# Feed-forward stage of a decoder layer: top-row products of the first pair ahead, splits in order of use, a place of its own for two gated blocks, and a down-projection over eight banks

## The reference, cut to what matters

```python
up = causal_dwconv(rms_norm(h, g_ffn[l]) @ w_up[l], w_conv[l], b_conv[l])   # 2 x 2816 channels, 3 taps
a, b = up[..., :D_FF], up[..., D_FF:]
h = h + (jax.nn.silu(a) * b) @ w_down[l]
return rms_norm(h, g_final)
```

## Time and profile before

| | us |
|---|---|
| median of 3 runs (lowest to highest) | 1912.57 (1912.17 to 1915.29) |
| the profiled execution, its own time | 1916.99 |
| its span in the trace | 1915.2 |
| TensorE busy | 1834.9 (96%) |
| VectorE, ScalarE, GpSimd busy | 951.7, 667.8, 953.6 |

### The profile page before, as it was taken

One profiled execution on the slowest core, in us unless ns is written; L12 is line 12 of the kernel. 1 busy time (PEld: TensorE's weight loads), 2 busy tenths in 40 slices (PEclk: granted clock), 3 DMA queues, 4 the chain that ended last, 5 costly groups with the idle time before them and its releaser, 6 DMA issues.

```text
span 1915.2 us, 25387 instructions
## 1 busy us (share of the span) xinstructions
PE 1834.9 (96%) x8924; PEld 1525.2 (80%) x8924; DVE 951.7 (50%) x1420; ACT 667.8 (35%) x1161; POOL 953.6 (50%) x519
## 2 busy tenths in 40 slices
PE   6999999999997999999999999899999999699998
PEld 6788888888886788878888877588888888588887
DVE  5355454000016566774345445677778787632212
ACT  6422223121013566621233223544444444322212
POOL 6833333456654776334532332567777777533220
PEclk9999999999998899999999999999999999899999
DMA  6511111353322887173221232234343433554312
GB/s 251 198 45 34 34 42 44 137 179 123 93 83 84 318 318 270 45 271 103 99 67 56 66 132 89 94 111 131 115 131 115 131 108 127 188 166 131 103 51 88
DMA packets 72667, 237.95 MB, mean 124 GB/s; under 512 B 6800, under 2 KB 17168, under 8 KB 69264
## 3 DMA queue, kind: packets, MB, share of 16 engines
q1 hardware_dynamic: 48720, 159.31, 25.5%
q10 hardware_dynamic: 23872, 77.60, 11.0%
HBM read 172.93 MB, written 63.96 MB: 124 GB/s over the span
## 4 chain that ended last, share of the span: by engine, by line
PE 64%; POOL 12%; issue 12%; DVE 5%; ACT 5%; DMA 1%; POOLq 0%; ACTq 0%; SPq 0%; DVEq 0%
PE ps L559 19%; PE ps L564 18%; PE ps L565 18%; POOL wl L488 8%; POOL zB L495 2%; PE ps L917 2%; ACT prow L1530 2%; PE ps L894 1%; PE ps L1215 1%; PE ps L1217 1%; PE ps L1216 1%; DVE aneg L2220 1%; DMA raw<-in_slabs 1%; POOL zA L495 0%; PE ps L1045 0%
## 5 line engine op out<-in xcount | busy, mean ns | idle before, releaser
L456 POOL TENSOR_SCALAR wh<-raw 128x1024 fp32r<-128x1024 f32 x76 | 211.7, 2786 | 533.4 <-PE ps L559 510.5
L559 PE MATMUL ps<-uh,wh 128*128 128x512 f32 (+1 forms) x576 | 228.6, 397 | 2.4 <-POOL wl L458 2.4
L565 PE MATMUL ps<-uh,wl 128*128 128x512 f32 (+1 forms) x576 | 225.5, 391 | 0.0
L564 PE MATMUL ps<-ul,wh 128*128 128x512 f32 (+1 forms) x576 | 225.1, 391 | 0.0
L458 POOL TENSOR_TENSOR wl<-raw,wh 128x1024 fp32r<-128x1024 f32 x76 | 183.0, 2408 | 6.3
L488 POOL TENSOR_TENSOR wl<-raw,wh 128x512 fp32r<-128x512 f32 x88 | 140.0, 1611 | 35.3 <-ACT wh L1228 35.3
L535 POOL TENSOR_TENSOR wl<-raw,wh 128x1024 fp32r<-128x1024 f32 x28 | 71.4, 2551 | 141.6 <-ACT wh L1228 141.6
L1907 DVE SCALAR_TENSOR_TENSOR ya<-zA,sm,ya 128x512 f32<-128x512 f32 x88 | 93.8, 1066 | 89.3 <-ACT ya L1762 80.8
L475 POOL TENSOR_TENSOR over_rings<-over_rings 128x512 f32<-128x512 f32 x88 | 113.4, 1289 | 44.1 <-DMA over_rings<-in_slabs 38.8
L1907 DVE SCALAR_TENSOR_TENSOR yb<-zB,sm,yb 128x512 f32<-128x512 f32 x88 | 127.7, 1451 | 14.4 <-ACT yb L1762 8.2
L1228 ACT ACTIVATE wh<-raw 128x512 fp32r<-128x512 f32 (+1 forms) x124 | 90.5, 749 | 115.3 <-PE ps L559 78.0
(11 more groups left out here) (434 smaller groups left out, 4855.4 us busy)
## 6 DMA issues: line engine op xcount, KB each, us to landing
raw<-in_slabs SPq DMA_DIRECT2D x134, 512.0 KB, 3.6
over_rings<-in_slabs SPq DMA_DIRECT2D x22, 1024.0 KB, 7.0
s_s<-over_rings SPq DMA_DIRECT2D x22, 1024.0 KB, 4.8
ssm<-s_s SPq DMA_DIRECT2D x22, 512.0 KB, 3.7
raw<-s_s SPq DMA_DIRECT2D x22, 512.0 KB, 4.7
s_f<-yb ACTq DMA_DIRECT2D x22, 512.0 KB, 2.6
fs<-s_f ACTq DMA_DIRECT2D x22, 512.0 KB, 3.5
a<-in_slabs SPq DMA_DIRECT2D x22, 256.0 KB, 2.6
```

What stands on the lines that cost most here:

```text
L456: pool.tensor_scalar(wh[:, j, :], raw[:, j % RAWS, :], 1.0, None, ALU.mult).then_inc(S["w_hi"], 1)
L559: l = pe.matmul(o, lh, rh, start=start, stop=False)
L564: pe.matmul(o, lh, rl, start=False, stop=False)
L565: return pe.matmul(o, ll, rh, start=False, stop=stop)
```

## The change

Five things are moved; no arithmetic is added or removed.

1. Pair 0 on TensorE: VA11 waits for bank 0 alone; VA12 comes second (both use f0), and the order is VA11, VA12, VS2, VS1, VS3, VS4, VA22. So that VA12 can be added into bank 0, TensorE waits for ScalarE's copy of VA11.
2. Before it, VectorE takes out half 0 of the last `w_xo` block ahead of `mixed(2)`, and the high parts and differences of t2, t1, t3, b2 and t4 are written out in one list each (HIS, LOS). t4's high parts no longer stand behind the copy of the 1/rms rows.
3. Gated blocks 4 and 5 get a staging tile fs4 of their own; their loads wait for VA12 of the last pair (fs4 lies on f0h). VectorE takes the differences of 0, 2, 3 and 4, GpSimd those of 1 and 5.
4. The down-projection uses all eight banks: block m is in banks 2(m mod 4) and the next. Group 0 computes blocks 0 to 3 of its operands for m = 0 and m = 1 first, then operands 4 and 5 for both (`first_two`). The waits for a free bank look three blocks back.
5. The wait for the last gated block's store goes from in front of the weight splits to the load of gated block 6. The transposes of the final gain are moved behind block 0 of group 2, into banks 4 and 5.

```diff
+FIRST = (VA11, VA12, VS2, VS1, VS3, VS4, VA22)
+HIS = [("t2", 0), ("t2", 1), ("t2", 2), ("t3", 0), ("t3", 1), ("t1", 0), ("t2", 3), ("t1", 1), ("t3", 2), ("t1", 2),
+       ("t3", 3), ("t1", 3), ("b2", 0), ("b2", 1), ("b2", 2), ("b2", 3), ("t4", 0), ("t4", 1), ("t4", 2), ("t4", 3)]
+LOS = [("t2", 0), ("t2", 1), ("t2", 2), ("t1", 0), ("t2", 3), ("t1", 1), ("t1", 2), ("t1", 3),
+       ("b2", 0), ("b2", 1), ("b2", 2), ("b2", 3)]
...
+        (fs4,) = place(72, [("fs4", [P, 2, T], 0)])
...
-            round_of(FB - 1, (lambda: (down(0), f_lo(1)), lambda: (f_lo(3), down(1))))
+            round_of(FB - 1, (lambda: (down(0), f_lo(1), down(1), f_lo(5)), lambda: None))
             scaled_by(FB, "zb0", zB, 0, v_at(FB, "c21"))
-            f_lo(5)
...
                 if first:
-                    for b in range(2):
-                        pe.wait_ge(d_free[b], FF_USE0)
-                elif second_:
+                    pe.wait_ge(d_free[0], FF_USE0)
+                    product(i, VA11, q, f0h, f0l, ready=made("o_gl", lambda k: KB + k + 1))
+                    pe.wait_ge(S["f_a"], a_at(0, "p1c"))
+                    product(i, VA12, q, f0h, f0l, CH, more=True, ready=made("o_gl", lambda k: KB + CH + k + 1))
+                    pe.wait_ge(d_free[1], FF_USE0)
+                    product(i, VS2, q + 1, t2h, t2l, ready=made("xT_lo", lambda k: lo_at("t2", k)))
+                    sums(1, ach, acl)
...
+            def first_two():
+
+
+                pe.wait_ge(S["f_v"], v_at(FB - 1, "c21"))
+                for ks in (range(CH), range(CH, FGROUPS[0])):
+                    for m in range(2):
+                        if ks[0] == 0:
+                            pe.wait_ge(S["w_ready"], s + m + 1)
+                        for b in range(2):
+                            for k in ks:
...
+                        if g == 0 and isinstance(i, int) and i == 0:
+                            pe.wait_ge(S["f_v"], v_at(FB - 1, "c12") if j == 2 else v_at(FB, "c21"))
+                            dense(j, s + j, 0, G, blocks(g), freed=2 if j == 2 else 1, bank=2 * j)
+                            continue
+                        if g == len(FGROUPS) - 2 and isinstance(i, int) and i == 0 and j == 2:
+                            pe.wait_ge(S["rb_c"], 3)
+                        dense(j, s + 4 * i + j, u + 4 * i + j - 3, G, blocks(g), bank=2 * j)
...
+                    if m == KB - 1 and b == 1:
+                        act.wait_ge(d_done[1], USE0["xo"] + KB)
+                        parts(0, 3)
                     square(1, m, b, USE0["xo"], hF, sq, f0h, "g_ffn")
...
+                if m == KB - 1:
+                    p1_copy(0, 0)
...
-                if c in (4, 5):
-                    act.wait_ge(*((S["f_p"], F_AT[1]) if c == 5 else (S["xT_lo"], 2 * KB + 3 * CH + 1)))
+                if c == 4:
+                    act.wait_ge(S["p_done"], NV * (FB - 1) + VA12 + 1)
+                elif c == 6:
+                    act.wait_ge(S["g_st0"], ST0 + 16 * FB)
...
             gated_out(FB)
-            act.wait_ge(S["g_st0"], ST0 + 16 * FB)
...
+            evac(0)
+            mixed(2)
...
-            quarters(n, 1, (lambda: f_lo(2, 0, 2),))
+            quarters(n, 1, (lambda: (f_lo(2, 0, 2), f_lo(3, 0, 3)),))
+            f_lo(4, 0, 4)
             rest_of(FB, 0)
-            f_lo(4, 0, 4)
```

More of the change, by code:

```diff
@@ L1126, in seven, with made @@
                 q = 4 * e
-                def made(sem_, n):
-                    return (lambda k: pe.wait_ge(S[sem_], n + k + 1)) if first else None
+                def made(sem_, at):
+                    return lambda k: pe.wait_ge(S[sem_], at(k))
                 def after(name, n=i):
@@ L1133, in seven @@
                 if first:
-                    for b in range(2):
-                        pe.wait_ge(d_free[b], FF_USE0)
-                elif second_:
+                    pe.wait_ge(d_free[0], FF_USE0)
[5 more added lines that the diff above has]
+                    sums(1, ach, acl)
+                    product(i, VS1, q + 2, t1h, t1l, ready=made("xT_lo", lambda k: lo_at("t1", k)))
+                    product(i, VS3, q + 3, t3h, t3l, ready=made("f_p", lambda k: k + 1))
+                    rms_rows(1)
+                    after("u4")
+                    product(i, VS4, q + 2, b2h, b2l, more=True, ready=made("xT_lo", lambda k: lo_at("b2", k)))
+                    after("c22")
+                    product(i, VA22, q + 3, t4h, t4l, more=True, ready=made("f_p", lambda k: CH + k + 1))
+                    return
+                if second_:
                     pe.wait_ge(S["rb_c"], 2)
@@ L1140, in seven @@
                     after("c21", i - 1)
[L1141 to L1148, removed]
+                product(i, VA11, q, f0h, f0l)
+                product(i, VS2, q + 1, t2h, t2l)
+                product(i, VS1, q + 2, t1h, t1l)
+                product(i, VS3, q + 3, t3h, t3l)
                 after("u2")
-                product(i, VA12, q, f0h, f0l, CH, more=True, ready=made("o_gl", KB + CH))
+                product(i, VA12, q, f0h, f0l, CH, more=True)
                 after("u4")
-                product(i, VS4, q + 2, b2h, b2l, more=True, ready=made("xT_lo", 2 * KB + 2 * CH))
+                product(i, VS4, q + 2, b2h, b2l, more=True)
                 after("c22")
-                product(i, VA22, q + 3, t4h, t4l, more=True, ready=made("f_p", CH))
+                product(i, VA22, q + 3, t4h, t4l, more=True)
             seven(0, 0)
@@ L1751, in _ @@
                            scale=1.0 / D, bias=cnc("eps")).then_inc(S["ss_s"], 1)
-            for k in range(CH):
-                x_part(("x_b", 2 * k + 2), b2h[:, k, :], hF[:, k + CH, H2:T] if k < 3 else bb3[:, :])
-            act.wait_ge(S["xT_lo"], 2 * KB + 2)
+            for v in (VA22,):
+                v_hi(0, v)
+            parts(4 * CH, 5 * CH)
+            act.wait_ge(S["xT_lo"], lo_at("t2", 3))
             rms_copy(1, rbF)
-            for k in range(CH):
-                x_part(("x_t", 4 * k + 4), t4h[:, k, :], hF[:, k + CH, 0:H2])
             def tap(i, name, c, x_, b, z, y):
@@ L1888, in _ @@
             for t in range(NT):
[L1889 removed]
+                p = 2 * (t % 4)
                 for b in range(2):
@@ new lines, in lows, with evac, accumulate @@
+            def lows(a, b):
+                for name, k in LOS[a:b]:
+                    l_, h_, full = los[name](k)
+                    dve.wait_ge(S["xT_hi"], hi_at(name, k))
+                    lo(l_[:, k, :], full, h_[:, k, :]).then_inc(S["xT_lo"], 1)
+            def evac(b):
+                dve.wait_ge(d_done[b], USE0["xo"] + KB)
+                dve.tensor_tensor(hF[:, KB - 1, half(b)], ps[:, b, :], hs[:, 1, half(b)], ALU.add).then_inc(d_free[b], 1)
+            def accumulate(b):
+                q = 4 * KB - 2 + b
+                dve.wait_ge(S["o_sq"], q + 1)
+                dve.wait_ge(S["o_ac"], q - 1)
+                dve.tensor_tensor(acc[:, b, :], acc[:, b, :], sq[:, b, :], ALU.add).then_inc(S["o_ac"], 1)
```

164 lines of the change are left out of this document (90 added, 74 removed).

## The result

The changed kernel takes 1894.76 us in the median of 4 runs (1888.76 to 1896.34), the kernel before 1913.55 (4 runs beside it, 1912.17 to 1915.29): ratio 0.9896, interval 0.9876 to 0.9916. It is faster by about 1%, and lies 6.8 us above the 1888.0 forecast and 1.3 us outside the range. The profiled execution took 1888.76 us, which is almost the 1888.0 forecast for the median, though the prediction gave 1892.4 for a profiled execution; the experiments show that the agreement is chance.

What follows compares the result with a forecast made beforehand. TensorE, busy 1834.9 of 1915.2 us, was taken as the bound, so only its waits and half-clock stretches could be won: 18.1 + 6.5 = 24.6 us, from 1912.57 to 1888.0, range 1884.5 to 1893.5.

Steps and rivals of the forecast that it cites:

- operand 3's wait: Down-projection's start: operand 3's difference, on VectorE behind operand 2's, comes slightly late; counted as 0.2 us.
- part one: Start of the down-projection: the new order removes TensorE's idle time and half clock there; 18.1 us, between 15 and 18.3.
- part two: Pairs 0 and 1 of the up-projection: earlier splits and new order gain 6.5 us, between 3 and 9.
- t4's end: Before pair 1: t4's last difference on GpSimd ends at 1221.8, between 1220 and 1224, 6.5 us sooner.
- Operands 4 and 5, weight slab 3: Down-projection: operands ready 2.6 us early, slab 3 with 1.2 us cover; rival that either is late, 1890 to 1893, chance 0.15.
- This edit gains nothing of itself: Eight banks in the down-projection: no gain of their own, since no row shows TensorE waiting for a bank there.
- The head: Start of pair 0: VA11 starts at once, but 2 of the 4.1 us return as a wait before VA12.
- 0.8 goes again: Pair 0: 0.8 us of t4's 6.5 is lost because VectorE's taps fall beside pair 1's weight splits.
- 0.8 of the 2.4 as won: VA12 of pair 1: of the 2.4 us that half clock cost its 12 matmuls, 0.8 is won.
- the start of pair 0 gains nothing: Rival, chance 0.16: VectorE and GpSimd collide more than counted at pair 0, leaving only the down-projection's gain; 1894.5 us.
- the slower case: Rival, chance 0.02: TensorE waits for u2 in all of pairs 2 to 21; 1928 us at 2 us a pair.
- The clock rival: Rival, chance 0.08: after shorter waits the clock stays high through both pairs, all 2.4 us come back; 1885 us.

Runs made afterwards that it cites:

- four_banks: The changed kernel with the down-projection in four banks instead of eight; its new wait costs 4.1 us and the slower clock behind it 2.8 us.
- shared_place: The changed kernel with gated blocks 4 and 5 loaded to the old staging place; first to 73rd down-projection matmul 17.19 us against 17.20.
- half1_first: The changed kernel with half 1 of the last w_xo block taken out right after mixed(2); last w_xo matmul to end 698.65 us.
- junction_only: The changed kernel's new down-projection, with pair 0's order, take-outs and splits as before the change; 1896.17 us, ratio 0.9913 to the kernel before.
- pair0_only: Only the change's parts at pair 0, with the down-projection as in the kernel before; 1910.30 us, ratio 0.9978 to the kernel before.
- one_by_one: The changed kernel with m = 0 done before m = 1 in group 0; first to 73rd down-projection matmul 22.24 us, 5.0 us more.

## Why the forecast missed

The direction, both places and the additivity of the two halves were right; the sizes and the base were not. The change is worth 21.0 us by the medians (1914.71 to 1893.73) and 20.9 to 22.3 by the marks, not 24.6. Four terms of the sum were mis-sized: operand 3's wait in part one, and in part two t4's end, the way from there to zA, and the clock.

- **Part one, 18.1 forecast.** B-C was forecast at 16.3 to 16.6 and is 17.20. The step that was too small is "Operand 3 ... I count 0.2 us". The two differences of operands 2 and 3 took 3.0 us each beside GpSimd, not the 2.68 of the earlier trace rows: this row of VectorE after is what operand 3 waited for:

```profile
1628.39 6.01 DVE L1969 TENSOR_TENSOR fal<-fs,fah 128x1024 fp32r<-128x1024 f32 x2
```

  The 10th matmul starts 0.93 us behind the 9th instead of 0.227, so the term is 0.7 and not 0.2. On the other side, 34.60 was not what the old kernel always takes: another profile has 33.45. Part one is worth 16.3 to 17.4.
- **Operands 4 and 5, weight slab 3.** Forecast ready 8.3 us after B; GpSimd's difference of 5 ended 8.5, VectorE's of 4 9.6 after it, when 10.9 was needed: not late. Slab 3's low part ends at 1656.08, 24.4 us after B, and is needed at 25.4. The cover of 1.2 us was 1.0; no wait.
- **"This edit gains nothing of itself".** Right against the kernel before, which waited for no bank; against the new order it is wrong: `four_banks` loses 6.9 us. The prediction had said that TensorE would stand with two banks, and put no price on it. The new place for blocks 4 and 5 is worth nothing (`shared_place`), so the load behind the difference in fs0, where the prediction saw the first cause, isn't what makes the new order fast. Its second and third cause, the copy behind silu and two taps and the difference behind four, fit the rows: the copies started 9.2 us after B before and start 4.1 after it now, and operand 4's difference ends 9.6 us after B for 18.0. No run takes these two reorderings apart.
- **The head.** VA11 starts at once (0.23 us after W), and 2.68 us of wait before VA12 are back, forecast 2. `f0l` took 1.78, beside GpSimd. That it costs nothing at the end was right as far as tested: `half1_first` removes the wait, gets another in its place and gains nothing.
- **Part two, 6.5 forecast, 4.7 to 4.9 measured.** t4's last difference came 6.2 us sooner (forecast 6.5). The largest error is in what lies between it and zA: "0.8 goes again" was 1.5, since two of pair 1's weight splits took 3.00 us and two more 3.55 beside VectorE, for some 2.5 a pair before. So VA12 of pair 1 came 4.7 us sooner, not 5.7 (3.7 against the profile of `junction_only`). The 2 us more at t4 that the prediction drew from the rule of mutual exclusion didn't come: t4 was 0.3 us late on the forecast.
- **The clock, "0.8 of the 2.4 as won".** This term failed by its mechanism. In the profile after the 12 matmuls of VA12 take 4.4 us (5.3 before, from 1245.04 to 1250.32), in the window from 1234 to 1239 at a granted clock of 0.66:

```profile
1234.00:1239.00 5.00, 4.71 (x13) 3.41 (x13) 4.83 (x7) 0.06 (x1) 2.36 (x2) 0.66 0.00 0
```

  That looks like the 0.8 forecast, but it is luck: other profiles have anything from none to all of it at this place, and it changes nothing in A-B. `pair0_only` and `shared_place` (columns as in the earlier trace rows):

```profile
1242.35:1247.00 4.65, 3.01 (x12) 2.17 (x12) 4.50 (x5) 0.00 (x0) 2.17 (x2) 1.00 0.00 0
```

```profile
1239.20:1244.40 5.20, 5.20 (x12) 4.12 (x13) 5.02 (x6) 0.47 (x1) 2.15 (x2) 0.50 0.02 9
```

  The first is at full clock throughout, the second at half; A-B is 397.66 and 397.56. What VA12 wins is lost in the wait for VectorE's u4 before VS4 of pair 1, which the prediction left out, 1.69 us in `pair0_only`:

```profile
1247.05 0.50 PE L1137 MATMUL ps<-b2h,wh 128*128 128x512 f32 x1 [1.69 <-DVE u L2523]
```

  In the profile after it is 0.25 us there, and this in pair 2:

```profile
1258.84 0.49 PE L1138 MATMUL ps<-b2h,wh 128*128 128x512 f32 x1 [0.61 <-DVE u L2550]
```

  From A to VS4 of pair 2 are 24.6 to 24.8 us in all kernels but the three with zA moved. So the clock gave A-B between 0.0 and 0.2 us, and part two is 4.7 to 4.9.
- **The base.** The sum was taken from 1912.57, the median of three runs. Twenty-three more of that kernel have a median of 1914.71. Of the 6.8 us between forecast and result, 3.6 are the sum (24.6 for 21.0; by the marks 0.7 to 1.8 of it in part one and 1.6 to 1.8 in part two), 2.1 are the base, and 1.0 is the difference between the two medians of the changed kernel. The range was built from costs inside the change alone, and held nothing for the 5 to 9 us by which executions of the same code differ.
- **The rivals.** That the start of pair 0 gains nothing gave 1894.5, near the result by its number, but not by its mechanism: `pair0_only` is faster by 4.4 us. No wait on weight slab 3 or on operands 4 and 5 is in the list. Pair 2 has the one short wait above and no later pair any, so the slower case didn't arise. The clock rival is refuted in both steps: shorter waits don't keep the clock here (half of VA12 and more is slow behind 2.88 us in `half1_first`, none behind 2.98 in `four_banks`), and where VA12 did run at 1.00 the time didn't fall.

## What to carry to other kernels

When the profiled time of one kernel varies from run to run by more than the disputed effect, subtract stretches between two marks in the same trace, the first one ahead of the change, and not spans; here that took the spread of the changed kernel from 5 us to 0.1, and that of the old one to 1.4. A profile whose total agrees with a forecast proves nothing until its stretches agree too. Two engines that keep each other from SBUF, as in the differences of b2 and t4 here (6.9 us side by side, 7.6 for the sum of both alone), should be planned for with the sum of their times, and such work moved to where the other one is idle. Before counting clock or a removed wait as won, look at which wait comes next: here the wait for u4 took back all that a faster VA12 had gained.

## What was not expected of the hardware

The same instructions ahead of the change took from 1188.42 to 1196.62 us in 14 profiles, and the stretch from 560 to 680 us is of one of two kinds, 0.94 or 0.90 to 0.91 of the clock, mostly with other waits in each. What decides between the two stays open; no run here was made for it. And the length of a wait didn't decide what clock followed it. At VA12 of pair 1, waits of 2.89 to 2.98 us were followed by no slow matmul in `pair0_only`, `one_by_one` and `four_banks`, and by seven 0.43 us apart in the profile after; one of 4.21 us by seven in `junction_only`, and by eleven in the profile before and its repeat.
